# Loading the transposed expert table in pairs of blocks in a one-core decoder layer

## The chip, the cores and the metric

The kernel runs on one core of one Trainium2 chip. The metric is the device time of one execution, in microseconds (us). The engines are TensorE (PE), VectorE (DVE), ScalarE (ACT), GpSimd (POOL) and SyncE (SP); SP only issues transfers here, and POOL issues the gathers.

## The reference

One decoder layer over 512 tokens of width 1024. A mixer (a state-space scan, stick-breaking attention and cross-attention to a memory, with one projection in and one out) is followed by a retrieval layer over 16,384 experts of one neuron each, and the latter is what the change touches:

```
q = (h @ wq) as 8 heads x 2 halves;  scores = q . keys       (128 keys per half)
top 16 of each half, top 16 of the 256 sums  ->  eidx, gates = softmax
act = gelu(u_tab[eidx] . h)                                  (one dot per expert)
out = sum over the 128 chosen experts of gate * act * v_tab[eidx]
```

Tables u and v hold 16,384 rows of 1024 values of 4 bytes.

## The kernel before, in words

The mixer runs first (up to about 300 us) and is left alone by the change. In the retrieval layer, tokens 0 to 127 are done by gathers: POOL gathers the chosen rows of u and later v, 128 tokens x 4 KB in each gather, through eight buffers (`urow`), and DVE makes one dot, or one accumulation, out of each (lines 479 to 502, 1760). The other 384 tokens are done densely. For each of the 128 blocks of 128 experts (NK = 128) PE computes all activations (the up projection, `up`, line 947), and later, block by block, multiplies activations by gates and by v (the down projection, `down`, line 1032). Sparse gates become dense arrays by one-hot products, built beside 48 of the up blocks (`gates`, line 970).

Up projection. The transposed table `uT` lies in memory as one 512 KB block per 128 experts: 128 rows of 4 KB, one to a partition. It is loaded into four slots of `uraw` (line 238). fp32 values are split into an upper half (`uhi`, ACT, line 1370) and a lower half (`ulo`, DVE, line 1758), both in four slots, and PE makes 24 matmuls of a block: 16 with the upper half, 8 with the lower. Two PSUM banks alternate; ACT makes the activation out of a finished bank into `act_s` (line 1377), and PE's block i waits until activation i-2 is made (line 951). SP stores it as `acts_scratch` (192 KB).

The order on each queue is written out by hand. SP (lines 376 to 401), for i = 0 to 123: wait until DVE has made lower half i (line 380), load block i+4 into the slot thus freed (line 382), wait for activation i-1 and store it (line 384), store a 2 MB chunk of dense gates where one is complete (line 386), and, at i = 113, 116, 119 and 122, load the first parts of `gring` (gates, the first two times), `aring` (activations) and `vraw` (table v) for the down projection (lines 387 to 400). The gates of the three tiles of 128 dense tokens are built beside blocks 20 to 35, 56 to 71 and 92 to 107 (HOT_AT), and a 2 MB chunk is stored each time four further blocks are done, directly in front of the load of an odd block (blocks 29, 33, 37 and 41 in the first tile).

ACT (lines 1420 to 1441), for i = 0 to 123: upper half i+2 (it waits for the load, line 1367), where gates are built the copy of a finished gates product into its stage (line 1407), activation i-1, and the weighing of the one-hot rows `hotB` that PE takes next (line 1396). DVE makes the lower halves between the steps of its routing work (`up_to`, line 1769).

The last four up blocks stand between pieces of the down projection (`LAST_U`, line 1044). To find a block's instruction in the trace, count the 128 instructions of a line: the n-th of line 354 (load), 1370 (upper half), 1377 (activation) is block n-1's.

Of the kernel before, what the change touches and what calls it, by code (L numbers as in the profile page):

```python
# [27 lines left out]
P = 128  # L28
D = 1024
DC = D // P  # L30
# [14 lines left out]
NK = 128  # L45
# [109 lines left out]
def trunk(nc, xT_d, x_d, memT_d, wch_d, wv_d, par_d, dtb_d, alog_d, g2row_d, wout_d, wq_d, keys_d,  # L155
# [5 lines left out]
    with ctx:  # L161
        def sem(name):
            return ctx.enter_context(nc.semaphore(name))
# [7 lines left out]
        def at(kib, name, shape, dt=F32):  # L171

            with ExitStack() as place:
                if kib:
                    place.enter_context(nc.sbuf_tensor(f"below_{name}", [P, int(kib * 256)], F32))
                return place.enter_context(nc.sbuf_tensor(name, shape, dt))
# [61 lines left out]
        uraw, uhi, ulo = at(63, "uraw", [P, 4, DC, P]), at(79, "uhi", [P, 4, DC, P], F32R), at(13, "ulo", [P, 4, DC, P], F32R)  # L238
# [32 lines left out]
        s = Signals()  # L271
# [2 lines left out]
        w_in = [sem(f"w_in{i}") for i in range(RING)]  # L274
        job_full = [sem(f"job_full{b}") for b in range(8)]
        job_free = [sem(f"job_free{b}") for b in range(8)]
        u_in = [sem(f"u_in{i}") for i in range(4)]
        v_in = [sem(f"v_in{i}") for i in range(4)]
        a_in = [sem(f"a_in{i}") for i in range(4)]
        g_in = [sem(f"g_in{i}") for i in range(2)]  # L280
# [32 lines left out]
        def _(sp):  # L313
# [36 lines left out]

            sp.wait_ge(s["o_full"], 2 * NT)

            def load_u(k, i):
                sp.dma_start(uraw[:, k], uT_d[i]).then_inc(u_in[k], 16)

            def store_act(k, i):

                sp.wait_ge(s["act_ready"], i + 3)
                sp.dma_start(acts_d[i], act_s[:, k, :]).then_inc(act_stored[k], 16)

            def store_gates(c):

                e = c % 2
                sp.wait_ge(s["g_free"], 4 * (c + 1) + 2)
                sp.dma_start(gates_d[:, c, :, :], stage[e][:]).then_inc(gate_stored[e], 16)

            def load_v(k, i):
                sp.dma_start(vraw[:, k, :], v_d[i]).then_inc(v_in[k], 16)

            def load_a(k, i):  # L370
                sp.dma_start(aring[k], acts_d[i]).then_inc(a_in[k], 16)

            def load_g(e, g):
                sp.dma_start(gring[:, e], gates_d[:, :, bass.ds(4 * g, 4), :]).then_inc(g_in[e], 16)
            chunk_at = {HOT_AT[c // CPT] + 4 * (c % CPT) + 3: c for c in range(CHUNKS_G)}
            for k in range(4):
                load_u(k, k)
            for i in range(NK - 4):

                sp.wait_ge(s["u_split"], i + 1)  # L380
                sp.sem_inc(s["slot_go"], 1)
                load_u(i % 4, i + 4)
                if i:
                    store_act((i - 1) % 4, i - 1)
                    if i - 1 in chunk_at:
                        store_gates(chunk_at[i - 1])
                k, now = divmod(i - FIRST_DOWN, 3)
                if now == 0 and 0 <= k < 4:
                    if k == 0:

                        sp.wait_ge(s["g_full"], 16 * DT + 2)
                        sp.wait_ge(s["routed_ready"], NT)
                        sp.wait_ge(s["sco_full"], 4 * NT)
                        for e in range(2):
                            sp.wait_ge(gate_stored[e], 16 * (CHUNKS_G // 2))
                    if k < 2:
                        load_g(k, k)
                    sp.wait_ge(act_stored[k], 32)
                    load_a(k, k)
                    load_v(k, k)  # L400
# [652 lines left out]
        def _(act):  # L1053
# [310 lines left out]

            def upper_u(i):

                act.wait_ge(u_in[i % 4], 16 * (i // 4) + 16)

                act.wait_ge(s["p1_done"], i + 1)
                a_(uhi[:, i % 4], uraw[:, i % 4], ACT.Copy).then_inc(s["uhi_ready"], 1)  # L1370
# [8 lines left out]
            def tile(i):  # L1379
                if i + AHEAD < NK:  # L1380
                    upper_u(i + AHEAD)
                if i:
                    activations(i - 1)
# [25 lines left out]
            for h in range(PH):  # L1409
                act.wait_ge(s["pq_full"], h + 1)  # L1410
                a_(pqT[:, h, :], psum[:, 4 + h % 4, 0:TD], ACT.Copy).then_inc(s["pq_ready"], 1)
                if WQ_EARLY + 2 <= h + 2 < PH:
                    upper_wq(h + 2)
                if h == PH - 3:
                    for i in range(AHEAD):
                        upper_u(i)
# [3 lines left out]
            for i in range(NK - 4):  # L1420
                if i in softs:
                    softmax(softs[i])
                for tt in range(DT):
                    n = i - HOT_AT[tt]
                    if n == -1:
                        if tt + 2 < NT:
                            for m in range(PH // 2):
                                key_scores(tt + 2, m)
                        routed_turned(tt)
                if i + AHEAD < NK:  # L1430
                    upper_u(i + AHEAD)
                for tt in range(DT):
                    n = i - HOT_AT[tt]
                    if 0 < n <= 16:
                        stage_gates(16 * tt + n - 1)
                if i:
                    activations(i - 1)
                for tt in range(DT):
                    n = i - HOT_AT[tt]
                    if -1 < n + 1 < 16:  # L1440
                        weigh(16 * tt + n + 1)
# [591 lines left out]
```

## Time and profile before

| what | before |
|---|---|
| time, median of 3 runs (lowest to highest) | 1515.56 us (1515.03 to 1516.24) |
| the profiled execution: its time / its span | 1511.39 us / 1509.7 us |
| busy PE / DVE / ACT / POOL | 98% / 78% / 46% / 20% |
| data moved, mean rate | 403 MB, 267 GB/s |
| loads of uraw from uT | 128 of 512 KB |
| loads of vraw from v | 128 of 512 KB |
| stores of activations / of gates | 128 of 192 KB / 12 of 2048 KB |

The span runs from the first to the last instruction of the profiled execution; the time has what lies around it as well. Busy PE counts matmuls whose ends are modelled, so 98% says that PE has work, not that it is at its peak. Start times in the rows are us from the start of the span. "[idle before <-releaser]" is how long the engine stood still ahead of an instruction, and what ended that.

### The profile page before, as it was taken

The numbers are of one execution on the slowest core, as the hardware profiler recorded it, in microseconds if no ns is written. First come the engines' busy times: TensorE is split into PE (matmuls) and PEld (weight loads), VectorE is DVE, ScalarE is ACT, GpSimd is POOL, SyncE is SP. The second block draws the span as 40 slices with busy tenths as digits, with TensorE's granted clock in tenths as the row PEclk, the third lists the DMA queues.
The fourth block names the chain that finished last, engine by engine and source line by source line (L and its number), as shares of the span: only waits on it lengthen the run. The fifth ranks groups of instructions, "written<-read, shape, count | busy, mean of one in ns | idle before, by whom it ended". The sixth has DMA issues, their size and how long they took to land.

```text
span 1509.7 us, 23443 instructions
## 1 busy us (share of the span) xinstructions
PE 1480.8 (98%) x7883; PEld 1298.7 (86%) x7883; DVE 1182.8 (78%) x2156; ACT 699.6 (46%) x1235; POOL 307.4 (20%) x296
## 2 busy tenths in 40 slices
PE   7999999989999999999999999999999999999998
PEld 4877756478999999999999999988888888888887
DVE  6454572889998999789998884687878878788885
ACT  5454661133457734677347753433333333333331
POOL 1000100014122301222022352242222222232210
PEclk9999999989999999999999999999999999999999
DMA  7120303038778986699777999999999999999994
GB/s 285 52 70 0 140 19 149 1 142 312 228 254 312 356 301 228 237 336 353 282 231 262 352 354 373 357 378 354 347 319 356 337 334 355 330 383 356 348 345 149
DMA packets 170145, 403.00 MB, mean 267 GB/s; under 512 B 14048, under 2 KB 95968, under 8 KB 168032
## 3 DMA queue, kind: packets, MB, share of 16 engines
q1 hardware_dynamic: 133216, 268.01, 49.6%
q0 software_dynamic: 36864, 134.23, 25.4%
q8 instruction: 27, 0.44, 0.1%
q14 instruction: 38, 0.31, 0.1%
HBM read 347.67 MB, written 54.53 MB: 266 GB/s over the span
## 4 chain that ended last, share of the span: by engine, by line
PE 93%; DVE 3%; DMA 2%; ACT 1%; issue 1%; SPq 0%; DVEq 0%; ACTq 0%
PE psum L508 58%; PE psum L1040 35%; DMA uraw<-in_uT 2%; DVE urow L1764 1%; DMA wring<-in_chunks 0%; DVE ulo L1758 0%; DVE x L1636 0%; PE psum L770 0%; DVE sco L1823 0%; ACT pr L1223 0%; DVE hlo L1746 0%; DVE itop L1821 0%; DVE wqlo L1753 0%; DMA acts_scratch<-act_s 0%; DVE mstat L1671 0%
## 5 line engine op out<-in xcount | busy, mean ns | idle before, releaser
L508 PE MATMUL psum<-hhi,uhi 128*128 128x384 f32 x1024 | 347.1, 339 | 2.1 <-ACT act_s L1377 2.1
L508 PE MATMUL psum<-hlo,uhi 128*128 128x384 f32 x1024 | 342.4, 334 | 0.0
L1453 ACT ACTIVATE vhi<-vraw 128x1024 fp32r<-128x1024 f32 x128 | 135.9, 1062 | 330.6 <-PE psum L1040 330.6
L486 POOL DMA_INDIRECT urow<-in_u,eidx x128 | 154.6, 1208 | 581.4 <-DVE urow L1764 413.7
L1040 PE MATMUL psum<-vhi,whi 128*128 128x512 f32 x768 | 236.6, 389 | 0.0
L1040 PE MATMUL psum<-vhi,wlo 128*128 128x512 f32 x768 | 236.5, 389 | 0.0
L1040 PE MATMUL psum<-vlo,whi 128*128 128x512 f32 x768 | 236.4, 389 | 0.0
L1960 DVE TENSOR_TENSOR vlo<-vraw,vhi 128x1024 fp32r<-128x1024 f32 x128 | 156.6, 1224 | 78.3 <-ACT vhi L1453 76.8
L486 POOL DMA_INDIRECT urow<-in_v,eidx x120 | 132.5, 1104 | 371.8 <-DVE acc L1966 370.8
L508 PE MATMUL psum<-hhi,ulo 128*128 128x384 f32 x1024 | 199.5, 336 | 3.1 <-DVE ulo L1758 3.1
L508 PEld LDWEIGHTS psum<-hhi,uhi 128*128 128x128 f32 x1024 | 192.6, 188 | 3.1 <-ACT uhi L1370 2.4
L508 PEld LDWEIGHTS psum<-hlo,uhi 128*128 128x128 f32 x1024 | 192.6, 188 | 0.2
L508 PEld LDWEIGHTS psum<-hhi,ulo 128*128 128x128 f32 x1024 | 180.3, 189 | 3.5 <-DVE ulo L1758 3.5
L1758 DVE TENSOR_TENSOR ulo<-uraw,uhi 128x1024 fp32r<-128x1024 f32 x128 | 156.1, 1222 | 33.4 <-ACT uhi L1370 24.4
L1040 PEld LDWEIGHTS psum<-vlo,whi 128*128 128x128 f32 x768 | 144.1, 188 | 30.0
L1040 PEld LDWEIGHTS psum<-vhi,wlo 128*128 128x128 f32 x768 | 144.1, 188 | 29.9
L1040 PEld LDWEIGHTS psum<-vhi,whi 128*128 128x128 f32 x768 | 144.1, 188 | 29.7
L1966 DVE SCALAR_TENSOR_TENSOR acc<-urow,wrow,acc 128x1024 f32<-128x1024 f32 x128 | 163.6, 1278 | 0.0
L1377 ACT ACTIVATE act_s<-psum 128x384 f32<-128x384 f32 x128 | 62.6, 489 | 212.7 <-PE psum L508 210.7
L1370 ACT ACTIVATE uhi<-uraw 128x1024 fp32r<-128x1024 f32 x128 | 134.9, 1056 | 48.6 <-DMA uraw<-in_uT 47.9
L1764 DVE SCALAR_TENSOR_TENSOR urow<-urow,h2row 128x1024 f32<-128x1024 f32 x128 | 153.5, 1220 | 0.3
L1396 ACT ACTIVATE hotB<-hotB,rT 128x128 f32<-128x128 f32 x384 | 117.1, 392 | 0.0
(294 smaller groups left out, 1826.5 us busy)
## 6 DMA issues: line engine op xcount, KB each, us to landing
uraw<-in_uT SPq DMA_DIRECT2D x128, 512.0 KB
vraw<-in_v SPq DMA_DIRECT2D x128, 512.0 KB
acts_scratch<-act_s SPq DMA_DIRECT2D x128, 192.0 KB
gates_scratch<-stage SPq DMA_DIRECT2D x12, 2048.0 KB
gring<-gates_scratch SPq DMA_DIRECT2D x32, 768.0 KB
aring<-acts_scratch SPq DMA_DIRECT2D x128, 192.0 KB
wring<-in_chunks SPq DMA_DIRECT2D x20, 512.0 KB, 4.5
wout<-in_wout SPq DMA_DIRECT2D x1, 4096.0 KB, 12.7
```

The source lines that it names most:

```text
L486: g.indirect_dma_start(urow[k], None, table, bass.IndirectOffsetOnAxis(eidx[:, n % HK:n % HK + 1], 0)).then_inc(row_in[k], 16)
L508: return nc.tensor.matmul(out, lhsT, rhs, start=start, stop=stop)
L1040: last = nc.tensor.matmul(psum[:, 2 + 2 * t + half, :], l_[:, k, t * P:(t + 1) * P], r_[:, k, half * 512:(half + 1) * 512], start=False, s ...
L1370: a_(uhi[:, i % 4], uraw[:, i % 4], ACT.Copy).then_inc(s["uhi_ready"], 1)
L1377: a_(act_s[:, i % 4, :], psum[:, i % 2, 0:TD], ACT.Gelu).then_inc(s["act_ready"], 1)
L1396: ins = a_(hotB[:, n % 2, i, :], hotB[:, n % 2, i, :], ACT.Copy, scale=rT[:, 2, 8 * (n % 16) + i:8 * (n % 16) + i + 1])
L1453: a_(vhi[:, k, :], vraw[:, k, :], ACT.Copy).then_inc(s["vhi_ready"], 1)
L1758: v.tensor_tensor(ulo[:, k], uraw[:, k], uhi[:, k].bitcast(F32), ALU.subtract).then_inc(s["u_split"], 1)
L1764: v.scalar_tensor_tensor(urow[k], urow[k], 1.0, h2row[:, 0, :], ALU.mult, ALU.mult, accum_out=dots[:, j:j + 1]).then_inc(s["dot_ready"], 1)
L1960: v.tensor_tensor(vlo[:, k, :], vraw[:, k, :], vhi[:, k, :].bitcast(F32), ALU.subtract).then_inc(s["v_split"], 1)
L1966: v.scalar_tensor_tensor(acc0[:], urow[r], wrow[:, bass.ds(i, 1)], acc0[:], ALU.mult, ALU.add).then_inc(s["vrow_free"], 1)
```

## The change

The table `uT` is laid out on the host so that two blocks of experts of one partition are neighbours (rows of 8 KB), and it is loaded two blocks at a time, 1 MB in one transfer, into slots 0 and 1 or slots 2 and 3 of the same four. SP issues such a load at odd i alone, after lower halves i-1 and i are made; it then holds blocks i+3 and i+4. Two semaphores take the place of four. Stores, their places and all other work stay as they are.

```diff
--- before.py
+++ after.py
@@ -274,7 +274,7 @@
         w_in = [sem(f"w_in{i}") for i in range(RING)]
         job_full = [sem(f"job_full{b}") for b in range(8)]
         job_free = [sem(f"job_free{b}") for b in range(8)]
-        u_in = [sem(f"u_in{i}") for i in range(4)]
+        u_in = [sem(f"u_in{i}") for i in range(2)]
         v_in = [sem(f"v_in{i}") for i in range(4)]
         a_in = [sem(f"a_in{i}") for i in range(4)]
         g_in = [sem(f"g_in{i}") for i in range(2)]
@@ -350,8 +350,8 @@
 
             sp.wait_ge(s["o_full"], 2 * NT)
 
-            def load_u(k, i):
-                sp.dma_start(uraw[:, k], uT_d[i]).then_inc(u_in[k], 16)
+            def load_pair(j):
+                sp.dma_start(uraw[:, 2 * (j % 2):2 * (j % 2) + 2], uT_d[j]).then_inc(u_in[j % 2], 16)
 
             def store_act(k, i):
 
@@ -373,13 +373,14 @@
             def load_g(e, g):
                 sp.dma_start(gring[:, e], gates_d[:, :, bass.ds(4 * g, 4), :]).then_inc(g_in[e], 16)
             chunk_at = {HOT_AT[c // CPT] + 4 * (c % CPT) + 3: c for c in range(CHUNKS_G)}
-            for k in range(4):
-                load_u(k, k)
+            load_pair(0)
+            load_pair(1)
             for i in range(NK - 4):
 
-                sp.wait_ge(s["u_split"], i + 1)
-                sp.sem_inc(s["slot_go"], 1)
-                load_u(i % 4, i + 4)
+                if i % 2:
+                    sp.wait_ge(s["u_split"], i + 1)
+                    sp.sem_inc(s["slot_go"], 1)
+                    load_pair(i // 2 + 2)
                 if i:
                     store_act((i - 1) % 4, i - 1)
                     if i - 1 in chunk_at:
@@ -1364,7 +1365,7 @@
 
             def upper_u(i):
 
-                act.wait_ge(u_in[i % 4], 16 * (i // 4) + 16)
+                act.wait_ge(u_in[i % 4 // 2], 16 * (i // 4) + 16)
 
                 act.wait_ge(s["p1_done"], i + 1)
                 a_(uhi[:, i % 4], uraw[:, i % 4], ACT.Copy).then_inc(s["uhi_ready"], 1)
@@ -2018,7 +2019,7 @@
         "g2row": np.broadcast_to(f(norm2_g), (P, D)),
         "wout": f(w_out), "wq": f(peer_wq),
         "keys": f(peer_keys).transpose(1, 3, 0, 2).reshape(P, PH, NK),
-        "uT": f(peer_u).reshape(NK, P, DC, P).transpose(0, 3, 2, 1), "u": f(peer_u), "v": f(peer_v).reshape(NK, P, D),
+        "uT": f(peer_u).reshape(NK // 2, 2, P, DC, P).transpose(0, 4, 1, 3, 2), "u": f(peer_u), "v": f(peer_v).reshape(NK, P, D),
     }
     nc = bacc.Bacc("TRN2", target_bir_lowering=False, num_devices=1)
     arrays, args = {}, []
```

## Rows read from the trace of the kernel before

**Rows 1.** the chain that ended last (section 4 of the page), shares by engine

```profile
PE 93%; DVE 3%; DMA 2%; ACT 1%; issue 1%; SPq 0%; DVEq 0%; ACTq 0%
```

**Rows 2.** stretches: us, busy PE PEld DVE ACT POOL, clock, DMA, GB/s

```profile
904.00:970.00 66.00, 63.88 (x367) 63.13 (x366) 33.01 (x43) 25.34 (x36) 12.97 (x13) 1.00 0.98 371
...
1210.00:1505.00 295.00, 295.00 (x1305) 244.34 (x1303) 234.49 (x280) 100.59 (x137) 61.97 (x61) 1.00 0.92 326
```

**Rows 3.** waits of the whole span: who, for whom, us in total, times, longest

```profile
ACT uhi L1370 <- DMA uraw<-in_uT: 47.9, 24, 8.3
```

**Rows 4.** the chain in order of time, 904 to 1040: start us, us, what

```profile
904.04 0.50 ACT act_s L1377
...
905.00 12.93 DMA uraw<-in_uT
...
918.92 0.48 ACT act_s L1377
...
922.37 11.40 DMA uraw<-in_uT
...
1035.61 4.18 PE psum L508 x24
```

**Rows 5.** timeline of ACT in a plain stretch: start us, us, what, [idle before]

```profile
565.65 1.05 ACT L1370 ACTIVATE uhi<-uraw 128x1024 fp32r<-128x1024 f32 x1
569.42 0.49 ACT L1377 ACTIVATE act_s<-psum 128x384 f32<-128x384 f32 x1 [2.72 <-PE psum L508]
```

**Rows 6.** timelines of SP, ACT and PE where gates are built (tile 1)

```profile
466.26 0.39 SPq L354 DMA_DIRECT2D uraw<-in_uT  x1
...
473.45 1.05 ACT L1370 ACTIVATE uhi<-uraw 128x1024 fp32r<-128x1024 f32 x1
...
476.67 0.49 ACT L1377 ACTIVATE act_s<-psum 128x384 f32<-128x384 f32 x1 [1.26 <-PE psum L508]
477.06 2.44 ACT L1396 ACTIVATE hotB<-hotB,rT 128x128 f32<-128x128 f32 x8
...
476.47 1.95 PE L508 MATMUL psum<-hotA,hotB 128*128 128x128 f32 x16
...
482.42 1.83 PE L508 MATMUL psum<-hotA,hotB 128*128 128x128 f32 x15
```

**Rows 7.** timelines of SP and ACT at the first two tiles' last gates

```profile
537.58 0.38 SPq L354 DMA_DIRECT2D uraw<-in_uT  x1
...
540.69 1.05 ACT L1370 ACTIVATE uhi<-uraw 128x1024 fp32r<-128x1024 f32 x1
...
549.61 1.06 ACT L1370 ACTIVATE uhi<-uraw 128x1024 fp32r<-128x1024 f32 x1 [4.65 <-DMA uraw<-in_uT]
...
718.48 0.37 SPq L354 DMA_DIRECT2D uraw<-in_uT  x1
...
728.44 1.06 ACT L1370 ACTIVATE uhi<-uraw 128x1024 fp32r<-128x1024 f32 x1 [2.59 <-DMA uraw<-in_uT]
```

**Rows 8.** DMA issues: what, count, KB each, median us to landing

```profile
wout<-in_wout SPq DMA_DIRECT2D x1, 4096.0 KB, 12.7
...
x<-in_x SPq DMA_DIRECT2D x1, 512.0 KB, 3.3
```

**Rows 9.** timelines of SP and ACT at the third tile's last gates

```profile
897.16 0.42 SPq L354 DMA_DIRECT2D uraw<-in_uT  x1
...
910.54 1.06 ACT L1370 ACTIVATE uhi<-uraw 128x1024 fp32r<-128x1024 f32 x1 [6.00 <-DMA uraw<-in_uT]
```

**Rows 10.** timelines of SP and ACT in the early blocks

```profile
385.92 0.33 SPq L354 DMA_DIRECT2D uraw<-in_uT  x1
...
388.54 0.49 ACT L1377 ACTIVATE act_s<-psum 128x384 f32<-128x384 f32 x1 [2.72 <-PE psum L508]
```

**Rows 11.** PE alone in two stretches: as rows 2, without the other engines

```profile
361.00:364.00 3.00, 0.50 (x3) 1.00 0.80 269
364.00:368.00 4.00, 3.35 (x11) 0.57 0.83 262
```

## Prediction

> **What bounds the kernel now.** I read the chain of waits first: it lies on TensorE (PE) for 93% of the span [rows 1]. A change of the loads can therefore cost or win time only where PE stands still. Next, the busy times by stretch: in the last part, where only down projections are left, PE is busy throughout and no uraw load is left to move; in the 66 us where the last blocks overlap the first loads of the down projection, PE is busy 63.9 of 66 at 371 GB/s [rows 2]. Then the waits: ScalarE (ACT) stood 47.9 us in 24 waits for uraw, of 128 loads [rows 3]. So today these loads are nearly always early, and where they are late the lateness is swallowed before it reaches PE. The exception is the chain's piece at 905 to 935, which runs over two uraw loads of 12.93 and 11.40 us [rows 4]; there PE lost 2.1 us (66.0 less 63.9).
>
> **How much cover a load has.** From the code: SP stores block i-1's activations only after it has issued the load of block i+4, and it stands in front of that store until ACT has made the activation. So every load comes just behind the activation of a block six numbers below it. The chain shows the steps: activation at 904.04, load issued at 905.00, landed, then 1.0 us of ACT (the upper half) until the next activation at 918.92 [rows 4]. I use 1.0 us before and 1.0 us behind each load.
> A block costs PE 4.18 us [rows 4]. In a plain stretch (no gates) block 46's upper half runs at 565.65, and the activation that follows it on ACT at 569.42, after 2.72 us of idleness [rows 5]. PE needs that activation only one block later, so a late upper half is free for 2.7 + (4.2 - 0.5 - 0.2) = 6.2 us. The whole loop (activation, load, upper half, activation two blocks on) must fit into two blocks, 8.3 us, if a pair is loaded per turn: the load may last 6.3 us.
> Where the gates are built, ACT has less room. Block 28's upper half runs at 473.45, then ACT idles 1.26 us before its activation at 476.67, and it has weighed hotB by 479.50 (477.06 + 2.44), which PE takes at 482.42 [rows 6]: a late upper half is free for 1.3 + 2.9 = 4.2 us. One block lasts 5.95 us there (476.47 to 482.42), four last 23.8.
>
> **What the change does to it.** Sixty-four SP issues go; nobody waits for SP's issue time, so that is 0. The extra slot_go counts are waited for by nobody: 0. Bytes, the work of ACT and DVE (VectorE) and the slots stay. What moves: the even block of each pair was loaded one iteration earlier than the odd one, in its own transfer. Now both are issued at the odd block's place, in 1 MB, and the even block's upper half has to wait for all of it. Its cover shrinks by one block, and its load grows.
>
> **Price of 1 MB.** 512 KB landed in 3.3 us and 4096 KB in 12.7 us [rows 8]: 9.4 us for seven more units, so 1.34 us for each further 512 KB when the queue has the DMA engines to itself. Beside the gathers of GpSimd it could get half: 2.7 us. I take 2.0. A lone 512 KB load lasts 3.3 us, or 4.7 if gathers take half its share too (3.3 + 1.34), so a pair lasts 4.6 to 7.4; I take 6.0.
> By the Trainium skill (DMA: Bandwidth & Descriptors, "Rules for kernel authors") the best bandwidth wants at least 1 MiB in a DMA, which speaks for the change; by its fit in "Anatomy of one DMA" (a constant of about 2.0 us, plus bytes over 436 GB/s) the pair would take an estimated 4.4 us and two singles 6.4. The rows agree with the saving (4.6 against 6.6), and by that rule alone the sum would be a gain wherever DMA bounds; but here the cover of a load counts, not its rate.
>
> **The stretches, one by one** (PE time lost):
> - Plain: 6.0 is under 6.3, so 0. At 7.4 it would be 1.1 us per pair, the second rival.
> - Early, blocks 6 to 19: the loads wait for DVE's lower halves. Pair (10, 11) would be issued at 385.92, land at 391.9 and let activation 7 be made at 392.9; made at 388.54 today, it is wanted 4.0 later, at 392.5 [rows 10]. 0.4 at some of seven pairs: 1.5 (0 to 4).
> - Gates: behind each 2 MB store of gates lies an odd block's load. At 466.26 it was issued [rows 6]; nothing there waited for it, so it lasted under 13.1 us (block 29's upper half, one block behind 473.45). At two tile ends such a load is waited for: 12.0 us (537.58 to 549.61) and 10.0 (718.48 to 728.44) [rows 7]. I take 10.0, nearest to a place where no one waited, and 12.0 for the pair. Block 28 then has it at 478.3 instead of 473.45: 4.8 late, 0.6 over the cover. The lateness that is left delays the next stores and loads; loop of four blocks: 1.5 (a second store is issued ahead of this load) + 12.0 + 2.0 (upper half and the gates' copy), then 1.0 + 6.5 + 2.0, 25.0 in all against 23.8, so 1.2 for each of the next two. 3.0 per tile, three tiles: 9 (0 to 30).
> - Ends of the first two tiles: pair (40, 41) is issued at 537.58 + 0.7, lasts 14.0 and is wanted at 540.69 [rows 7]: 11.6 late less 6.2 free = 5.4. At the second, 10.0 + 2.0 = 12.0 gives 3.4. Together 8.8 (5 to 16).
> - The last eight pairs, from the third tile's end. (112, 113): block 113's load at 897.16 was taken at 910.54, 13.4 us [rows 9]; with 2.0 more it lands at 912.6, activation at 913.5. PE wants that one, which now ends at 904.5, by 908.0 (3.5 us of cover, as above), and waits 5.5. (114 to 117): 6 us each, no wait. (118, 119), a little behind gring, aring and vraw: 8.0, wait 1. (120, 121): now right behind the next gring, aring and vraw, as block 118 was for 11.40 [rows 4]: 13.4, and only 5 of it covered: wait 9. (122 to 125): 0.5. (126, 127), behind aring and vraw: 6.0 to 13.4, taken as 9.5; here ACT begins the down projection's halves only afterwards, so PE waits 7 to 8. The sum is 23.5; less today's own delays, 2.1 of standing and as much again that I allow for: about 20 (9 to 30).
> - Clock: PE was busy 0.5 of the 3 us up to 364, and the stretch 364 to 368 has a granted clock of 0.57 [rows 11], mostly the lower level, 1.2 GHz: 4 us of matmuls at 0.57, so 1.7 lost. Two tile ends would pay that, 3.4; in the last stretch slower matmuls fall into time in which loads are late anyway.
> - DVE and POOL: the lower halves are behind the upper ones on DVE, with its routing work between; DVE waits later than ACT does, and the gathers follow DVE. What hides this is PE's own wait for the same block. I take 0; if that cover is gone (a lower half late at its matmul), the same lateness counts once more, in the upper bounds.
> Sum: 1.5 + 9 + 8.8 + 20 + 3.4 = 42.7. It is made against the profiled execution, 1511.39 us (span 1509.7), 4 us below the median of the runs, 1515.56. I put it onto the median: 1558.
>
> **Rivals.**
> 1. The end is not slower: the saving of fixed time decides. It would act where DMA is the wait, from 904 to 970, by ending PE's 2.1 us; the point from which it decides is a pair that lands, behind its neighbours, no later than today's two singles would let PE go on, about 5 us of cover. For it: 371 GB/s there [rows 2] and the page's rule. Against: the loads' cover in rows 6 and 7 is shorter than the loads behind a store. It gives 1513.5; chance 0.10, nearly all of it within 0.2% (3.0 us, about what a measurement of this kernel tells from no change).
> 2. The loads bound PE in the plain stretches too: pairs of 7.4 us make a loop of 9.4 against 8.3, 1.1 us at some 26 pairs, 28 more: 1586. For it: ACT waits already in early blocks. Chance 0.17.
> 3. Little but the last stretch loses: SP's queue has the DMA engines nearly to itself when a pair is wanted, and each costs 1.34 more and no further; gates 1, tile ends 5 with no clock loss, last pairs 10, so 16: 1532. For it: the free time between loads in the plain stretches. Against: 371 GB/s in the last. Chance 0.15.
> 4. Forecast: 0.58. That the rows don't become 8 KB I exclude: the array is laid out so that two blocks of a partition are neighbours.
>
> **The range** runs from a little below the third rival (16 with its last pairs at half, 11), 1527, to a little above the second, 1590. Slower by over 0.2%: 0.89; within: 0.08; faster: 0.03.
>
> **What would show it.** ACT's wait for uraw rises from 47.9 to well over 150 us; PE waits for act_s near the blocks behind the gates' stores, most at the two tile ends and from 905 to 990; the first down matmul moves from 970 to about 1010; the down part keeps its length. PE's busy share by stretch stays 100% in the plain ones. The forecast is wrong if uraw pairs land in under 5 us in the plain stretches and under 11 behind a store, or if PE waits in the plain stretches at all.

## The result, and the profile after

| | before | after |
|---|---|---|
| time, median (lowest to highest) | 1515.9 us (1515.03 to 1519.88, 4 runs) | 1550.4 us (1546.12 to 1552.91, 4 runs) |
| ratio, 95% interval | 1 | 1.0229 (1.0208 to 1.0249) |
| span of the profiled execution | 1509.7 us | 1551.2 us |
| mean granted clock of that execution | 0.995 | 0.983 |

The change costs 34.5 us. The forecast was 1558 us (1527 to 1590), slower with a chance of 0.89.

The page of the kernel after, in the lines that answer to [rows 1] and to the table of before (busy shares, the chain by engine, and the issues of uraw):

```profile
PE 1498.3 (97%) x7883; PEld 1312.3 (85%) x7883; DVE 1182.1 (76%) x2156; ACT 697.4 (45%) x1235; POOL 304.3 (20%) x296
...
PE 76%; DMA 11%; DVE 4%; issue 4%; ACT 3%; SPq 1%; DVEq 0%; ACTq 0%
...
uraw<-in_uT SPq DMA_DIRECT2D x64, 1024.0 KB
```

PE's share of the chain fell from 93% to 76%, and DMA's rose from 2% to 11%: the chain now runs through loads of uraw. The busy share of PE hardly moved (98% to 97%), so by that line alone one would not have found the loss.

The list of waits of the kernel after (who waited for whom, us in total, times, longest). The first line answers to [rows 3]; the second is ACT waiting for PE, its spare time, which was 210.7 us in 108 waits in the kernel before:

```profile
ACT uhi L1371 <- DMA uraw<-in_uT: 199.8, 49, 13.6
...
ACT act_s L1378 <- PE psum L509: 102.7, 62, 7.2
```

ACT waits for 49 of 64 pairs, where it waited for 24 of 128 loads, and for 200 us in place of 48. Most of it came out of ACT's spare time; PE stood still for 24 us of it, in the stretches below. These are all of PE's own idle stretches over 1 us between blocks 10 and 124 (timeline of PE, kernel after; the idle time stands in brackets), and the last line is the first down matmul:

```profile
406.99 0.41 PE L509 MATMUL psum<-hhi,uhi 128*128 128x384 f32 x1 [1.16 <-ACT act_s L1378]
...
561.39 0.66 PE L509 MATMUL psum<-hhi,uhi 128*128 128x384 f32 x1 [5.84 <-ACT act_s L1378]
...
748.06 0.66 PE L509 MATMUL psum<-hhi,uhi 128*128 128x384 f32 x1 [2.65 <-ACT act_s L1378]
...
936.74 0.66 PE L509 MATMUL psum<-hhi,uhi 128*128 128x384 f32 x1 [7.43 <-ACT act_s L1378]
...
966.80 0.41 PE L509 MATMUL psum<-hhi,uhi 128*128 128x384 f32 x1 [2.16 <-ACT act_s L1378]
...
979.89 0.49 PE L509 MATMUL psum<-hhi,uhi 128*128 128x384 f32 x1 [4.53 <-ACT act_s L1378]
...
1009.96 0.74 PE L1041 MATMUL psum<-vhi,whi 128*128 128x512 f32 x2 [1.91 <-DVE wlo L1963]
```

Those of 5.84, 2.65 and 7.43 us stand where a pair was issued right behind a gate store, before blocks 39, 75 and 111, at the three tiles' ends; those of 2.16 and 4.53, before blocks 117 and 119, stand behind loads for the down projection. The first matmuls behind the three last 0.66 us in place of 0.41, and the table of stretches shows why: the granted clock had fallen. Busy times by stretch, kernel after (us, busy PE, PE's weight loads, DVE, ACT, POOL, then granted clock, DMA share, GB/s):

```profile
560.00:567.00 7.00, 5.61 (x18) 5.64 (x19) 5.90 (x25) 2.64 (x5) 0.00 (x0) 0.52 0.64 209
745.00:752.00 7.00, 4.35 (x17) 4.06 (x16) 4.29 (x21) 2.77 (x4) 0.00 (x0) 0.76 0.73 255
...
937.00:943.00 6.00, 6.00 (x21) 6.00 (x21) 3.90 (x6) 1.57 (x3) 2.12 (x2) 0.54 0.88 296
...
904.00:970.00 66.00, 56.41 (x321) 55.81 (x319) 33.30 (x47) 22.23 (x35) 21.34 (x17) 0.92 0.87 316
```

The first three follow the three stand-stills: the granted clock is about a half, the lower level of 1.2 GHz, in all or part of the stretch. The last line answers to [rows 2]: PE is busy 56.4 of 66 us in place of 63.9, and the DMA engines move 316 GB/s in place of 371. On average they were less busy and the kernel slower, which speaks against bandwidth as what it lacked; the experiments that move transfers test that.

**Where the time went, by stretch.** From both traces I took the start of the first matmul of up blocks 0, 20, 36, and so on, and of the down projection; a column is by how much the stretch between two of them grew against the kernel before, in us. The first column is the mixer, which no kernel here touches. Each row is one profiled execution, and most are not at their kernel's median: that of "two halves, one wait" was 9 us under it (1543.4 to 1552.6).

| kernel | mixer | 0-20 | gates 20-36 | end 36-44 | 44-56 | 56-72 | end 72-80 | 80-92 | gates 92-108 | 108-124 | to down | down |
|---|---|---|---|---|---|---|---|---|---|---|---|---|
| after | 4.3 | 1.9 | 0.7 | 8.7 | 0.0 | 0.3 | 4.4 | 0.0 | 0.8 | 16.6 | 2.1 | 1.7 |
| late singles | 1.4 | 0.5 | 0.0 | 4.1 | 0.0 | 0.0 | 1.5 | 0.0 | 0.0 | 7.3 | 2.6 | 1.6 |
| 1 MB, 4 KB rows | 3.7 | 1.5 | 1.2 | 8.8 | 0.0 | 0.9 | 3.7 | 0.0 | 0.4 | 17.5 | 0.8 | 0.1 |
| store behind | 4.3 | 2.0 | 0.0 | 0.0 | 0.0 | 0.0 | 0.0 | 0.0 | 0.0 | 10.8 | 2.4 | 1.7 |
| down loads behind | 3.8 | 3.9 | 1.0 | 8.7 | 0.0 | 0.3 | 4.6 | 0.0 | 1.1 | 10.9 | 1.7 | 0.0 |
| both behind | 1.3 | 2.2 | 0.0 | 1.9 | 0.0 | 0.0 | 0.0 | 0.0 | 0.0 | 4.5 | 1.1 | 0.1 |
| two halves, one wait | -0.1 | 1.5 | 0.6 | 6.2 | 0.0 | 0.5 | 3.0 | 0.0 | 2.6 | 17.5 | 0.0 | 0.0 |
| before, store behind | 4.4 | 0.1 | 0.0 | 0.0 | 0.0 | 0.0 | 0.0 | 0.0 | 0.0 | -1.7 | 0.0 | 0.0 |

The mixer's 4.3 us are not the change's: the last kernel shows 4.4 there, and its median is that of the kernel before. Without them the spans differ by 37.2 us, near the 34.5 of the medians. In between, the up projection has grown by 35.5 us (all columns from 0-20 to the one before down). The 1.7 us of the down projection are the clock's, behind the 1.91 us for which PE waited ahead of it (PE alone, kernel after):

```profile
1010.00:1014.00 4.00, 4.00 (x11) 0.60 0.57 188
```

### The profile page after: what moved, and what is told of

It reads as the page before. It is cut to its first block, busy times and chain, and to the rows that moved or that the text cites. A ratio compares the mean times of both kernels' runs of the same rounds, so it can differ in the third digit from the quotient of the medians.

```text
span 1551.2 us, 23317 instructions
## 1 busy us (share of the span) xinstructions
PE 1498.3 (97%) x7883; PEld 1312.3 (85%) x7883; DVE 1182.1 (76%) x2156; ACT 697.4 (45%) x1235; POOL 304.3 (20%) x296
## 4 chain that ended last, share of the span: by engine, by line
PE 76%; DMA 11%; DVE 4%; issue 4%; ACT 3%; SPq 1%; DVEq 0%; ACTq 0%
PE psum L509 42%; PE psum L1041 34%; DMA uraw<-in_uT 11%; ACT act_s L1378 1%; DVE urow L1765 1%; ACT hotB L1397 1%; DMA xT<-in_xT 1%; ACT stage L1408 1%; DVE ulo L1759 0%; SPq L359 0%; DVE sco L1824 0%; DVE xlo L1492 0%; DVE itop L1828 0%; DVE itop L1822 0%; DVE rsB L1501 0%
## 5 line engine op out<-in xcount | busy, mean ns | idle before, releaser
L509 PE MATMUL psum<-hhi,uhi 128*128 128x384 f32 x1024 | 352.9, 345 | 23.9 <-ACT act_s L1378 23.9
L509 PE MATMUL psum<-hlo,uhi 128*128 128x384 f32 x1024 | 347.5, 339 | 0.0
L509 PEld LDWEIGHTS psum<-hhi,uhi 128*128 128x128 f32 x1024 | 196.5, 192 | 26.5 <-ACT uhi L1371 26.0
L509 PEld LDWEIGHTS psum<-hlo,uhi 128*128 128x128 f32 x1024 | 196.5, 192 | 0.2
```

The source lines that it names most:

```text
L509: return nc.tensor.matmul(out, lhsT, rhs, start=start, stop=stop)
```

## The experiments

The theory: the even block of each pair lost a block's lead, and then waits for a second half megabyte as well; PE pays where a pair is issued behind other transfers. The rivals: the size or the layout of the transfer itself, the lead alone, and the DMA engines' rate. Each ratio below is against 14 or 20 runs of the kernel before that were taken for the experiments (medians 1513.6 and 1514.1 us), and not against the 1515.9 us of the table above.

**Late singles.** The old table and 128 loads, with the even block's at the pair's place:

```diff
 for i in range(NK - 4):
-    sp.wait_ge(s["u_split"], i + 1)
-    sp.sem_inc(s["slot_go"], 1)
-    load_u(i % 4, i + 4)
+    if i % 2:
+        sp.wait_ge(s["u_split"], i + 1)
+        sp.sem_inc(s["slot_go"], 1)
+        load_u((i - 1) % 4, i + 3)
+        load_u(i % 4, i + 4)
```

> The kernel before, its 4 KB rows and its 128 loads of 512 KB, but the even block's load is issued at odd i, just ahead of the odd one's, where the change issues its pair. Theory (the even block lost its lead of one block, and besides waits for a second half megabyte): most of the loss is here already. The even block lands 1 to 2 us sooner than a pair did, so the early blocks lose 0.5 us instead of 2, the two tile ends about 8 instead of 13, the last blocks about 12 instead of 18: 1.014 times the kernel before (1.009 to 1.019), uraw waits of ACT 120 to 170 us. Rival A (the transfer's size alone is the cost): 1.000. Rival B (only the lead counts, the size nothing): 1.023, as the change.

Measured: 1527.4 us, 1.0086 (1.0059 to 1.0113), ACT's waits for uraw 145.7 us. Both pure rivals fall: neither the size alone (1.000) nor the lead alone (1.023) gives this. My size of it was too high, 1.014 with 1.009 as its low end. PE's stand-still at the first tile end, and the waits (both of this kernel):

```profile
552.68 0.41 PE L510 MATMUL psum<-hhi,uhi 128*128 128x384 f32 x1 [2.27 <-ACT act_s L1379]
```

```profile
ACT uhi L1372 <- DMA uraw<-in_uT: 145.7, 46, 10.5
```

2.27 us in place of 5.84, and 46 waits among 128 loads in place of 49 among 64. By the ratios the lead is worth about 13 us of the 34.5 and the second half megabyte about 21; by the stretches, mixer left out, 17.6 and 19.6 of 37.2. So the split is known to some 5 us.

**Two halves, one wait.** The same two loads of the old table at the same place, but both upper halves wait for both. The lines removed are those of the change:

```diff
-sp.dma_start(uraw[:, 2 * (j % 2):2 * (j % 2) + 2], uT_d[j]).then_inc(u_in[j % 2], 16)
+for e in range(2):
+    sp.dma_start(uraw[:, 2 * (j % 2) + e], uT_d[2 * j + e]).then_inc(u_in[j % 2], 16)
...
-act.wait_ge(u_in[i % 4 // 2], 16 * (i // 4) + 16)
+act.wait_ge(u_in[i % 4 // 2], 32 * (i // 4) + 32)
```

> The change in two transfers of 512 KB at the pair's place, in the old layout, where both upper halves wait for both. Against the late singles (1.009) it differs only in that the even block waits for the odd one's half megabyte too; against the change only in the transfer being cut in two. Theory (the wait for the second half megabyte is what the size costs): as the change, 1.023 (1.019 to 1.026). Rival A' (one large transfer is itself slower or takes more from others than two small ones): as the late singles, 1.009 to 1.013.

Measured: 1552.6 us, 1.0254 (1.0224 to 1.0284), with PE standing still 4.39, 2.77, 7.12, 2.49 and 4.76 us at the places of the change. Two of them in its timeline, and then block 46's pair in a plain stretch (SP, ACT):

```profile
555.06 0.41 PE L510 MATMUL psum<-hhi,uhi 128*128 128x384 f32 x1 [4.39 <-ACT act_s L1379]
...
930.33 0.66 PE L510 MATMUL psum<-hhi,uhi 128*128 128x384 f32 x1 [7.12 <-ACT act_s L1379]
```

```profile
570.37 0.85 SPq L355 DMA_DIRECT2D uraw<-in_uT  x2
...
575.77 1.06 ACT L1372 ACTIVATE uhi<-uraw 128x1024 fp32r<-128x1024 f32 x1 [1.73 <-DMA uraw<-in_uT]
```

The block was taken 5.4 us behind the first issue; in the late singles, which wait for the first half alone, it was 4.0 (568.00 to 572.04). So what the size costs is the wait for the odd block's bytes, and not the large transfer. Against the late singles this kernel differs only in what the upper halves wait for, and that made 25 us (1552.6 less 1527.4), where the change as a whole is 23 us above the late singles (1550.4 less 1527.4).

**1 MB in rows of 4 KB.** The change with the old table:

```diff
-sp.dma_start(uraw[:, 2 * (j % 2):2 * (j % 2) + 2], uT_d[j]).then_inc(u_in[j % 2], 16)
+sp.dma_start(uraw[:, 2 * (j % 2):2 * (j % 2) + 2], uT_d[2 * j:2 * j + 2].rearrange("b p c e -> p b c e")).then_inc(u_in[j % 2], 16)
```

> The change with the old table: 1 MB in one transfer at the same places, but in 256 rows of 4 KB instead of 128 of 8 KB. Theory: a row's length changes nothing, since the time depends on when all of 1 MB has landed: 1.023 times the kernel before (1.020 to 1.026), pairs behind nothing landing in 4.9 to 5.2 us as in the change. Rival C (rows of 8 KB go through less or more well, or take another share beside the gathers' rows of 4 KB): at least 0.005 away from the change, and the lone pairs at least 0.5 us away.

Measured: 1549.6 us, 1.0236 (1.0193 to 1.0280). Block 46's pair, issued in a plain stretch, was taken 5.2 us later (timelines of SP and ACT of this kernel), where the change took 5.0:

```profile
577.30 0.39 SPq L354 DMA_DIRECT2D uraw<-in_uT  x1
...
582.49 1.06 ACT L1371 ACTIVATE uhi<-uraw 128x1024 fp32r<-128x1024 f32 x1 [1.50 <-DMA uraw<-in_uT]
```

The length of the rows costs and gives nothing that can be measured.

**The layout alone.** The table in pairs, each block loaded by itself at the places of the kernel before:

```diff
-sp.dma_start(uraw[:, k], uT_d[i]).then_inc(u_in[k], 16)
+sp.dma_start(uraw[:, k], uT_d[i // 2][:, i % 2]).then_inc(u_in[k], 16)
```

> The other half alone: the table laid out in pairs, but each block loaded by itself (512 KB, rows of 4 KB at a pitch of 8 KB) at the places of the kernel before. Theory: 1.000 (0.998 to 1.002). Rival D (the layout in memory costs): 1.01 or more, with lone loads well over 3.5 us.

Measured: 1515.2 us, 1.0010 (0.9994 to 1.0026), and 0.1 us or less in every stretch behind the mixer but the last up blocks (1.1). Within 0.3%, the upper end of the interval, the layout is free.

**Store behind.** The change, with eleven gate stores one iteration later:

```diff
+if i - 2 in chunk_at and chunk_at[i - 2] < CHUNKS_G - 1:
+    store_gates(chunk_at[i - 2])
 if i:
     store_act((i - 1) % 4, i - 1)
-    if i - 1 in chunk_at:
-        store_gates(chunk_at[i - 1])
+    if chunk_at.get(i - 1) == CHUNKS_G - 1:
+        store_gates(CHUNKS_G - 1)
```

> The change, with eleven of the twelve 2 MB gate stores issued one iteration later, right behind the pair instead of right ahead of it (the last one stays, and so does the last stretch). Theory: the stalls at the first two tile ends (5.8 and 2.7 us, each followed by TensorE at half its clock, 13 us in all) and the small ones beside the gates (about 1.5) go, the last blocks' 18 and the early 2 stay: 1.014 (1.011 to 1.017). The pairs at 546 and 735 land in 5 to 7 us instead of 13.4 and 11.4. Rival E (the bytes bound there, whichever comes first): the wait only moves to the next pair, at least 1.020.

Measured: 1530.3 us, 1.0110 (1.0077 to 1.0143), at the better end of what was expected. PE alone over all the stretches up to the last gate store (busy, clock, DMA share, GB/s), and the pair at the first tile end (SP, then ACT), all of this kernel:

```profile
380.00:900.00 520.00, 518.32 (x3306) 1.00 0.80 289
```

```profile
543.36 0.36 SPq L354 DMA_DIRECT2D uraw<-in_uT  x1
543.77 0.45 SPq L365 DMA_DIRECT2D gates_scratch<-stage  x1
...
550.58 1.06 ACT L1373 ACTIVATE uhi<-uraw 128x1024 fp32r<-128x1024 f32 x1 [3.52 <-DMA uraw<-in_uT]
```

The pair takes 7.2 us with the store behind it, against 13.4 with the store ahead; PE stands still 1.7 us in 520, all of it in the early blocks. The wait did not move to the next pair: that one now took 8.8 us (552.49 to 561.27, where the change took 5.2), and PE did not stand still for it. ACT still waited 164 us for uraw in all, and between 380 and 900 nearly all of it was free. In the last stretch, too, this kernel lost 6 us less than the change (10.8 to 16.6): PE stood still 4.17 us before block 111 in place of 7.43, none before block 117 and 4.80 before block 119. Why the end of the third tile, whose last store was not moved, is better too was not tested; its earlier pairs were no longer late.

**Down loads behind.** The change, with the down projection's first loads at i = 113, 117, 119 and 123 in place of 113, 116, 119 and 122:

```diff
+DOWN_AT = [113, 117, 119, 123]
...
-k, now = divmod(i - FIRST_DOWN, 3)
-if now == 0 and 0 <= k < 4:
+k, now = DOWN_AT.index(i) if i in DOWN_AT else -1, 0
+if k >= 0:
```

> The change, with the second and the fourth group of first loads for the down projection (gring, aring, vraw) moved from i = 116 and 122, right ahead of a pair, to 117 and 123, right behind one. Theory: pair (120, 121) lands about 6 us after its issue instead of 9.2, so the 4.5 us that TensorE stood still before block 119 and the half clock behind it go, and the last pair lands sooner; the 5.8, 2.7 and 7.4 us behind the gate stores stay: 6 to 8 us less than the change, 1.018 times the kernel before (1.015 to 1.021). Rival E (bytes bound the last stretch, in whatever order): no gain, 1.023.

Measured: 1541.7 us, 1.0166 (1.0138 to 1.0195). Pair (120, 121), first issued and then taken, in this kernel:

```profile
968.08 0.36 SPq L355 DMA_DIRECT2D uraw<-in_uT  x1
...
973.30 1.06 ACT L1372 ACTIVATE uhi<-uraw 128x1024 fp32r<-128x1024 f32 x1 [4.37 <-DMA uraw<-in_uT]
```

5.2 us in place of 9.1, and PE no longer waits before block 119. A wait of 1.72 us before block 121 is new: the pair behind this one, (122, 123), was 9.6 us on the way (975.22 to 984.77), where the change's took 5.5; the moved loads are ahead of it now.

**Both behind.** All twelve gate stores and the four groups of first down loads (i = 115, 117, 119, 123) right behind a pair:

```diff
+DOWN_AT = [115, 117, 119, 123]
...
+if i - 2 in chunk_at:
+    store_gates(chunk_at[i - 2])
 if i:
     store_act((i - 1) % 4, i - 1)
-    if i - 1 in chunk_at:
-        store_gates(chunk_at[i - 1])
-k, now = divmod(i - FIRST_DOWN, 3)
-if now == 0 and 0 <= k < 4:
+k, now = DOWN_AT.index(i) if i in DOWN_AT else -1, 0
+if k >= 0:
```

> The change, with all twelve gate stores one iteration later, right behind a pair, and the four groups of first down loads at i = 115, 117, 119 and 123, right behind a pair too. Theory: nearly all the loss was in pairs that were issued behind other transfers. Of it the early blocks' 2 us stay and 1 to 3 in the last stretch: 1.003 times the kernel before (1.000 to 1.007). Rival E (bytes bound the last stretch): it keeps its 18 us, 1.010 or more.

Measured: 1522.5 us, 1.0052 (1.0034 to 1.0070). The largest idle times that PE still has between blocks 10 and 124 (timeline of PE of this kernel):

```profile
404.16 0.41 PE L510 MATMUL psum<-hhi,uhi 128*128 128x384 f32 x1 [1.55 <-ACT act_s L1379]
...
561.99 0.41 PE L510 MATMUL psum<-hhi,uhi 128*128 128x384 f32 x1 [1.65 <-ACT act_s L1379]
...
940.48 0.41 PE L510 MATMUL psum<-hhi,uhi 128*128 128x384 f32 x1 [0.82 <-ACT act_s L1379]
...
951.98 0.41 PE L510 MATMUL psum<-hhi,uhi 128*128 128x384 f32 x1 [2.94 <-ACT act_s L1379]
```

About four fifths of the loss (27.9 of 34.5 us by the medians, 1550.4 less 1522.5) were pairs behind other transfers in SP's queue. What is left stands in the early blocks (2.2 us), at the first tile's end (1.9) and from block 108 on (5.6). That it is the pair's own lack of lead is likely and was not tested by itself. Nor were the loads for the down projection moved in the kernel before, as the stores are in the next run; for them, that the move helps only because of the pairs is argued.

**Before, store behind.** The edit of "store behind", made to the kernel before:

```diff
+if i - 2 in chunk_at and chunk_at[i - 2] < CHUNKS_G - 1:
+    store_gates(chunk_at[i - 2])
...
```

> The kernel before, with eleven of its gate stores one iteration later, behind the odd block's load. Theory: its loads of 512 KB had enough lead, so ACT's waits for uraw at the two tile ends (4.7 and 2.6 us) go and TensorE gains nothing: 1.000 (0.998 to 1.002). Rival F (the stores' place matters for its own sake, for example by what they do to the gathers): 0.99 or less here too, and then what the store's place gave back in the change was not the pair's.

Measured: 1513.2 us, 0.9987 (0.9970 to 1.0004), no difference that these runs can tell, as expected. So the stores' place is worth something only where pairs are loaded. ACT's waits of 4.65 us for block 41 and 2.59 us for block 77 are gone, but one of 2.71 us for block 42 is new, and its waits for uraw hardly fell in all (42.8 us from 47.9). PE's 2.12 us of stand-still at 935 are gone from this profile, and 1.7 us of its last stretch with it; whether that is a gain is open.

## Why the prediction was right

**The mechanism** is the one argued: the up blocks' loads lost cover, ACT's waits quadrupled, PE paid at the places named, and nothing in the plain stretches. The first down matmul was forecast at about 1010 and came at 1009.96, 4.3 us of which are the mixer's. Two things came otherwise: the down part, said to keep its length, was 1.7 us longer by its clock (0.1 in the kernel with rows of 4 KB), and the last stretch lost 4.8 us to the clock, which I had put at nothing (below). Point by point, with the terms in us of PE time:

| step of the prediction | forecast | measured in the stretch |
|---|---|---|
| price of a lone pair in a plain stretch | 6.0 (4.6 to 7.4) | 5.0 (577.72 to 582.75) |
| plain stretches | 0 | 0.0, 0.0 |
| early blocks | 1.5 | 1.9 |
| gates beside the blocks | 9 | 1.8 (0.7 + 0.3 + 0.8) |
| first two tile ends, with their clock | 8.8 + 3.4 | 13.1 (8.7 + 4.4) |
| last pairs | 20 | 18.7 (16.6 + 2.1) |
| sum | 42.7 | 35.5 |

Of the signs that would have shown the forecast wrong, none appeared, one by a hair: pairs in the plain stretches mostly landed in 4.8 to 5.2 us (the sign was under 5), those behind a store in 11.1 to 14.5 (under 11). The lone pair is seen in the timelines of SP and ACT of the kernel after; the other two lines are the pair behind the first tile's last gate store:

```profile
577.72 0.36 SPq L354 DMA_DIRECT2D uraw<-in_uT  x1
...
582.75 1.06 ACT L1371 ACTIVATE uhi<-uraw 128x1024 fp32r<-128x1024 f32 x1 [1.34 <-DMA uraw<-in_uT]
...
546.42 0.43 SPq L354 DMA_DIRECT2D uraw<-in_uT  x1
...
559.81 1.06 ACT L1371 ACTIVATE uhi<-uraw 128x1024 fp32r<-128x1024 f32 x1 [12.05 <-DMA uraw<-in_uT]
```

**The term that was mis-sized** is "Gates": 9 us, of which 1.8 were found. Block 28's pair there, in the kernel after:

```profile
472.48 0.38 SPq L354 DMA_DIRECT2D uraw<-in_uT  x1
...
483.77 1.06 ACT L1371 ACTIVATE uhi<-uraw 128x1024 fp32r<-128x1024 f32 x1 [3.95 <-DMA uraw<-in_uT]
485.64 0.48 ACT L1378 ACTIVATE act_s<-psum 128x384 f32<-128x384 f32 x1
486.01 2.45 ACT L1397 ACTIVATE hotB<-hotB,rT 128x128 f32<-128x128 f32 x8
488.35 1.05 ACT L1371 ACTIVATE uhi<-uraw 128x1024 fp32r<-128x1024 f32 x1
```

It took 11.3 us where I had 12.0, and ACT stood idle 3.95 for it, just inside the cover of 4.2. The loop that I had at 25.0 us against 23.8 took 23.79 (472.48 to 496.27, the issues of pairs (28, 29) and (32, 33)): from the first issue to that of pair (30, 31) it was 14.1 where I had 15.0, and from there 9.7 where I had 10.0, with no wait for that pair at all. A sum at the edge of a cover turns on tenths of a microsecond, and I had charged the overrun nine times, for three chunks of each of three tiles; its bound, 0 to 30, held.

**The last stretch** came out near its sum by luck: several errors cancel. Pair (112, 113) lasted 14.5 (15.4 forecast) and PE stood still 7.4 rather than 5.5; (118, 119) cost 2.2 rather than 1; (120, 121) 4.5 rather than 9, since it lasted 9.1 and not 13.4; the wait ahead of the down projection was 1.9 rather than 7 to 8, since the last pair landed 8.5 us behind its issue, not 9.5, while PE, held up itself, had work for 10.8 us behind that issue (997.26 to 1008.05). Together PE stood still 16.0 us where I had 23.5. I then took off 4.2 for today's own delays, of which the kernel before shows 2.1 as standing; and I put the clock at nothing here, because slower matmuls would fall into time in which loads are late anyway. That step failed: 18.7 us less the 13.9 of additional standing leaves 4.8, and the clock was at about a half in two parts of the stretch in which PE was busy throughout (0.54 from 937 to 943, in the table of stretches, and this one, PE alone, kernel after):

```profile
980.00:984.00 4.00, 4.00 (x15) 0.57 0.84 233
```

**The clock.** 3.4 us were forecast at two tile ends. There the records show half clock from 560 to 567 and for half of the stretch from 745 to 752, and the two ends' 13.1 us less the 8.5 of standing (5.84 and 2.65) leave 4.6. The length of a stand-still does not tell by itself whether the clock falls: in the kernel after it fell behind 2.65 us and behind 1.91, in the late singles behind 2.27, and it stayed behind 2.12 us in the kernel before and behind 3.43 in the kernel with rows of 4 KB (its timeline, then its stretch, PE alone):

```profile
749.00 0.41 PE L509 MATMUL psum<-hhi,uhi 128*128 128x384 f32 x1 [3.43 <-ACT act_s L1378]
```

```profile
749.00:756.00 7.00, 7.00 (x40) 1.00 0.63 208
```

**The rivals.** The first (DMA's fixed time saved) is refuted by the first two experiments: two singles and one pair at the same place, with the same wait, cost the same, and the last stretch grew. By the rule in the Trainium skill (DMA: Bandwidth & Descriptors, "Rules for kernel authors") a DMA wants at least 1 MiB for the best bandwidth; no run here shows that gain. A lone pair landed in 5.0 us, less than twice the 3.3 of one single [rows 8], but two singles issued together had both landed in 5.4, and not in the 6.6 of the prediction. The other estimate from that page, 4.4 us, rests on a fit that the page gives for transfers issued by GpSimd; these are issued by SP. The second needed pairs over 6.3 us in the plain stretches; they lasted 5.0. The third put the tile ends at 5 us with no fall of the clock, and 13.1 were found; it put the last pairs at 10, and 18.7 were found; its 1 us for the gates was nearer the 1.8 than my 9. The price of a pair, too, came out nearer its 4.6 than my 6.0.

## What to carry to other kernels

Before two loads are merged, count the lead of the earlier one: it loses the time between the two issues, and it then waits for the last byte of both, so a slot ring of four becomes a ring of two. What a late load costs depends on what stands ahead of it in its queue; here moving a 2 MB store behind a load, an edit of a few lines, gave back all that the merging had cost beside the gates and at the first two tiles' ends. Rate and landing time are different things: the slower kernel had the less busy DMA engines.

## What the runs showed of the hardware that was not expected

A transfer of 1 MB in 128 rows of 8 KB, in 256 rows of 4 KB, or in two transfers of 512 KB took about the same time to land in full: 5.0, 5.2 and 5.4 us for block 46's pair in a plain stretch, the last with 0.4 us between its two issues. All three kernels have the same ratio within what these runs tell, 1.0229, 1.0236 and 1.0254 with intervals that overlap.

The mixer, which comes first and is the same in all these kernels, lasted up to 4.4 us longer in some profiled executions than in that of the kernel before, and where it was longer the granted clock was a little lower (PE alone over the first 200 us of the kernel before, and then of the store-behind version of it):

```profile
0.00:200.00 200.00, 189.52 (x944) 1.00 0.28 103
```

```profile
0.00:200.00 200.00, 189.42 (x928) 0.98 0.28 103
```

So the span of a single profiled execution carries some 4 us that are not the change's. Leaving the mixer out helps, but not wholly: the change and its version in rows of 4 KB, whose times agree, differ by up to 1.6 us in a stretch behind it.

A stand-still of PE of 1.91 us was followed by half clock in one kernel, and one of 3.43 us in another was not.
